# The last LayerNorm's weight and bias split by columns between VectorE and GpSimd

## What is computed

```python
def layer_norm(x, g, b):
    xf = x.astype(jnp.float32)
    mu = xf.mean(-1, keepdims=True)
    var = jnp.square(xf - mu).mean(-1, keepdims=True)
    return ((xf - mu) * lax.rsqrt(var + LN_EPS) * g.astype(jnp.float32) + b.astype(jnp.float32)).astype(x.dtype)
...
    x = layer_norm(ALPHA * x + moe(x, w_router, router_bias, w_exp_gu, w_exp_down, w_sh_gu, w_sh_down),
                   ln2_g, ln2_b)
```

## Time and profile before

| what | value |
|---|---|
| median of 3 runs | 2234.34 us (2234.02 to 2237.89) |
| the profiled execution | 2235.89 us |
| its span | 2234.1 us |
| busy in the span: TensorE, VectorE, ScalarE, GpSimd | 2070.3, 1078.4, 505.5, 550.4 us |
| last TensorE work ends, about | 2177.5 us into the span |
| the stage of the change | 2190.9 to 2230.0 us into the span |

### The profile page before, as it was taken

How to read it: one execution, slowest core, us unless ns; L and a number is a source line. 1 busy time by engine, 2 the same in 40 slices (tenths; PEclk the granted TensorE clock), 3 DMA queues, 4 the chain that set the end, 5 groups by cost and what they waited for, 6 DMA issues and landing times.

```text
span 2234.1 us, 24260 instructions
## 1 busy us (share of the span) xinstructions
PE 2070.3 (93%) x8178; PEld 1165.8 (52%) x8178; DVE 1078.4 (48%) x2232; ACT 505.5 (23%) x1011; POOL 550.4 (25%) x964
## 2 busy tenths in 40 slices
PE   8999698999998999998999898999999999999990
PEld 6755265655564656556555454444444444444440
DVE  5205599999998578963145553111111111111115
ACT  2314442000023652022022200111111111111122
POOL 0088860100031000100032243122222222222224
PEclk9999899999998999998999999999999999999995
DMA  4160004101010002104412141799999999999995
GB/s 129 46 68 3 1 4 151 38 19 47 1 31 18 1 1 57 43 15 151 137 55 68 38 160 52 277 367 370 371 366 368 366 364 367 367 368 368 371 337 176
DMA packets 126739, 365.20 MB, mean 163 GB/s; under 512 B 30849, under 2 KB 78722, under 8 KB 108866
## 3 DMA queue, kind: packets, MB, share of 16 engines
q1 hardware_dynamic: 106066, 290.21, 35.0%
q0 software_dynamic: 20016, 72.88, 12.9%
q10 hardware_dynamic: 576, 1.05, 0.1%
HBM read 310.82 MB, written 53.04 MB: 163 GB/s over the span
## 4 chain that ended last, share of the span: by engine, by line
PE 60%; DVE 23%; POOL 6%; issue 6%; ACT 2%; DMA 2%; SPq 0%; POOLq 0%; DVEq 0%; ACTq 0%
PE psum L817 21%; PE psum L831 10%; DVE arena L1672 9%; DVE best L1671 8%; PE psum L683 8%; PE psum L701 6%; PE psum L809 3%; PE psum L754 3%; ACT arena L1241 2%; PE psum L618 2%; PE psum L637 2%; POOL sct L1100 2%; PE psum L604 2%; PE psum L745 2%; POOL arena L1102 2%
## 5 line engine op out<-in xcount | busy, mean ns | idle before, releaser
L1241 ACT ACTIVATE arena<-psum 128x256 f32<-128x256 f32 (+8 forms) x714 | 334.4, 500 | 1517.8 <-PE psum L817 445.3
L817 PE MATMUL psum<-arena 128*128 128x512 f32 x1088 | 480.4, 594 | 1.1 <-DVE arena L1953 1.1
L817 PEld LDWEIGHTS psum<-arena 128*128 128x128 f32 x1088 | 202.7, 191 | 230.6 <-issue 229.4
L545 PE MATMUL psum<-arena 128*128 128x384 f32 (+1 forms) x768 | 238.9, 472 | 13.9 <-DVE arena L1697 8.4
L1671 DVE MAX8 best<-arena 128x8 f32<-128x384 f32 (+6 forms) x224 | 246.6, 1101 | 6.1
L1958 DVE TENSOR_TENSOR arena<-arena,psum 128x256 f32<-128x256 f32 x68 | 28.6, 421 | 454.6 <-ACT arena L1241 454.6
L831 PE MATMUL psum<-arena 128*128 128x512 f32 x544 | 244.8, 593 | 0.5 <-ACT arena L1241 0.5
L1672 DVE MATCH_REPLACE8 arena<-best,arena 128x384 f32<-128x384 f32 (+6 forms) x224 | 242.8, 1084 | 0.0
L545 PEld LDWEIGHTS psum<-arena 128*128 128x128 f32 x768 | 145.6, 191 | 106.8 <-DVE arena L1697 15.8
L1200 POOL TENSOR_TENSOR carry<-ones 1x1 f32<-1x1 f32 x135 | 52.1, 386 | 568.2 <-DVE arena L1967 521.1
L683 PE MATMUL psum<-arena 128*128 128x384 f32 (+1 forms) x576 | 179.1, 474 | 5.8 <-DMA arena<-in_w_attn_proj 5.8
(11 more groups left out here) (249 smaller groups left out, 2351.2 us busy)
## 6 DMA issues: line engine op xcount, KB each, us to landing
arena<-in_w_exp_gu SPq DMA_DIRECT2D x69, 2048.0 KB, 8.8
arena<-in_w_exp_down SPq DMA_DIRECT2D x68, 1024.0 KB, 7.4
arena<-in_w_in SPq DMA_DIRECT2D x24, 512.0 KB, 4.5
arena<-in_x_prompt SPq DMA_DIRECT2D x10, 512.0 KB, 4.1
arena<-in_w_glu SPq DMA_DIRECT2D x16, 256.0 KB, 5.0
arena<-in_w_attn_proj SPq DMA_DIRECT2D x16, 256.0 KB, 4.6
arena<-in_w_out SPq DMA_DIRECT2D x1, 4096.0 KB, 13.0
x_d<-arena SPq DMA_DIRECT2D x8, 512.0 KB, 2.9
```

Source lines behind the costliest of these rows:

```text
L545: last = mm(psum[:, b, 0:n], wgs[:, d % 2, w0 + k, :], src[:, k, t0:t0 + n], start=k == 0, stop=k == nk - 1)
L817: last = mm(psum[:, 2, :], xgT[u][:, k, :], ewg[u][:, k, :], start=k == 0, stop=k == DK - 1)
L1241: return act.activation(dst, src, fn, **kw)
```

## The change

The nine multiplies on VectorE and the nine adds on GpSimd, over all 1024 columns each, go. In their place VectorE does multiply and add on columns 0 to 383 of each tile (`weight_left`), and GpSimd does multiply and add on columns 384 to 1023. Both wait for `normed`, not for each other; each has a `step` between its two operations. SyncE waits for `out_left` and `out_right` before it stores a tile.

```diff
--- before.py
+++ after.py
@@ -78,6 +78,7 @@
 MASK_W = sum(keys(j)[1] for j in range(NT))
 TOK_CHUNKS = [(0, 384), (384, 384), (768, 320)]
 CHOOSING = list(range(2, NT))
+BY_VECTOR = 384
 
 
 class Banks:
@@ -1046,7 +1047,8 @@
                 ld(x1[0:rows(i), i, :], acc_d[tok(i), :], f"acc_loaded{i}")
 
             for i in range(NT):
-                sp.wait_ge(s("out_ready"), i + 1)
+                sp.wait_ge(s("out_left"), i + 1)
+                sp.wait_ge(s("out_right"), i + 1)
                 ld(out["y_p"][0, tok(i), :] if i < NT - 1 else out["y_s"][0], x1[0:rows(i), i, :], "out_stored")
             sp.wait_ge(s("out_stored"), 16 * NT)
             sp.wait_ge(s("v_stored"), 16 * NT)
@@ -1230,9 +1232,10 @@
 
             pool.wait_ge(s("ln2_loaded"), 32)
             for i in range(NT):
-                y = x1[0:rows(i), i, :]
-                pool.wait_ge(s("scaled"), i + 1)
-                tt(y, y, ln2[0:rows(i), 1, :], ALU.add).then_inc(s("out_ready"), 1)
+                r, y = rows(i), x1[0:rows(i), i, BY_VECTOR:]
+                pool.wait_ge(s("normed"), NT + i + 1)
+                step(tt(y, y, ln2[0:r, 0, BY_VECTOR:], ALU.mult))
+                tt(y, y, ln2[0:r, 1, BY_VECTOR:], ALU.add).then_inc(s("out_right"), 1)
 
 
         @block.scalar
@@ -1988,12 +1991,13 @@
                 dve.wait_ge(s(f"acc_loaded{i}"), 16)
                 variance(x, r, NT + i)
 
-            def scale_by_weight(i):
-                x = x1[0:rows(i), i, :]
+            def weight_left(i):
+                r, x = rows(i), x1[0:rows(i), i, 0:BY_VECTOR]
                 if i == 0:
                     dve.wait_ge(s("ln2_loaded"), 32)
                 dve.wait_ge(s("normed"), NT + i + 1)
-                tt(x, x, ln2[0:rows(i), 0, :], ALU.mult).then_inc(s("scaled"), 1)
+                step(tt(x, x, ln2[0:r, 0, 0:BY_VECTOR], ALU.mult))
+                tt(x, x, ln2[0:r, 1, 0:BY_VECTOR], ALU.add).then_inc(s("out_left"), 1)
 
             for i in range(NT + 2):
                 if i < NT:
@@ -2001,7 +2005,7 @@
                 if 0 <= i - 1 < NT:
                     scale_shift(rows(i - 1), NT + i - 1)
                 if 0 <= i - 2 < NT:
-                    scale_by_weight(i - 2)
+                    weight_left(i - 2)
 
 
 # ---- launch: one core; inputs and outputs as the reference has them ----
```

## The result

| | before | changed |
|---|---|---|
| median of 8 runs each, us | 2236.11 (2232.89 to 2241.6) | 2244.70 (2237.38 to 2248.83) |
| profiled execution, us | 2235.89 | 2245.38 |
| span, us | 2234.1 | 2243.5 |
| last stage, from tile 0's norm to the last operation, us | 35.45 | 40.30 |

The ratio is 1.0033, with a 95% interval of 1.0017 to 1.0048: slower by 7.4 us (3.8 to 10.7), where the forecast was 5.1 slower, a time of 2239.4 and a range up to 2242.4. The sign is right, the measured time lies 2.3 us above the range.

The account below looks back on a forecast made before the run. The prediction took GpSimd to set the last LayerNorm's pace by holding VectorE's one-column SCALAR_TENSOR_TENSOR. Steady tiles +6.62 and tail -1.53 gave +5.1 us, 2241.0 against the profiled execution, 2239.4 after its 1.55 us excess over the median; range 2235.8 to 2242.4.

Parts of the forecast that it names:

- The stage: Last LayerNorm, from tile 0's norm to the last VectorE or GpSimd operation: +6.62 - 1.53 = +5.1 us.
- The request of the small instruction: One-column SCALAR_TENSOR_TENSOR asks for the port 0.24 us after the gap between GpSimd's passes closes; held through the add.
- The period: Time per steady tile of the last LayerNorm: 4.50 us against 3.57, GpSimd waiting for ScalarE's norm.
- The VectorE pair: VectorE's multiply and add on the left 384 columns run beside ScalarE's norm, hidden with 0.30 us to spare.
- The steady tiles: Seven periods from tile 0's norm to tile 7's in the last LayerNorm: a loss of +6.62 us.
- The tail: From tile 7's norm to the last operation: 9.04 us against 10.57, VectorE and GpSimd in turn, gain -1.53 us.
- a rule for VectorE instructions with two inputs: A VectorE instruction with two SBUF inputs and a GpSimd one reading SBUF exclude each other for the whole instruction.
- How the numbers follow: Closing step giving chances for the whole time: slower by over 0.2% 0.60, within 0.2% 0.37, faster 0.03.
- something elsewhere in the program or the scatter of the runs: Case outside the last LayerNorm's terms, with runs of 2234.02 to 2237.89 us before: chance 0.03.
- The port is packed: Rival: the one-column SCALAR_TENSOR_TENSOR always finds the gap between GpSimd's passes; +1.8 us, 2236.1; packed or partly packed, chance 0.23.
- No exclusive hold: Rival: VectorE and GpSimd each run at their own pace, period 3.36 us; -4.3 us, 2230.0; chance 0.03.
- Worse than the sum: Rival: GpSimd's 640-column operation at 1.66 us, or VectorE losing every final turn; +6 to +8 us; chance 0.11.

Follow-up runs that it names:

- 640: The changed kernel with VectorE taking 640 columns and GpSimd 384, against the kernel before: ratio 0.9984 (0.9975 to 0.9993), stage 32.45 us.
- 512: The changed kernel with 512 columns each on VectorE and GpSimd, against the kernel before: ratio 1.0003 (0.9991 to 1.0014), stage 36.08 us.
- 640, one input: VectorE 640 columns, GpSimd 384, one-column SCALAR_TENSOR_TENSOR rewritten as TENSOR_SCALAR, against the kernel before: ratio 0.9986 (0.9974 to 0.9998), stage 32.32 us.
- 704: The changed kernel with VectorE taking 704 columns and GpSimd 320, against the kernel before: ratio 0.9970 (0.9955 to 0.9985), stage 32.68 us.
- the padded one: The kernel before plus nine tiny memsets ending each of VectorE's and GpSimd's streams and a second wait per store: ratio 1.0005 (0.9993 to 1.0017).

## Why the prediction was wrong, and where it was right

**The stage: right.** GpSimd's operation at 640 columns was put at 1.53 us and measured 1.53. The request of the small instruction was put 0.24 us behind the gap between GpSimd's passes; it came 0.23 behind the second pass's start. The period was put at 4.50 and measured 4.51. The VectorE pair hides, with 0.30 us to spare forecast and 0.29 measured. The steady tiles were put at +6.62: +6.79; 0.08 of the rest lie in the first period, 4.58, and 0.09 in the other six.

**The tail: right in kind, 0.4 us off, and the order was another.** It was put at -1.53 and is -1.94. The last small instruction is not held (0.15 us), as the text said. But VectorE's multiply of tile 7 got the port ahead of GpSimd (2232.09 against 2232.13), so the last operation is GpSimd's, not VectorE's. And I had charged four turns of 1.53 + 0.40. A full turn takes 1.80, as the ends at 2235.85, 2237.65 and 2239.45 show: VectorE 0.41, and GpSimd 1.39 from VectorE's end, so 0.14 of the 1.53 seem to pass inside the wait.

Sum of the stage: +4.85 for a forecast of +5.1. The two parts missed by 0.17 and 0.41 us in opposite directions, so the sum is a little closer than they are.

One reading goes further than its rows. The prediction says that the earlier trace rows agree with a rule for VectorE instructions with two inputs. The TENSOR_TENSOR there does; the CAST has one input and was held too, which the rule as the prediction words it doesn't give. For the forecast this changed nothing, since the stage has no CAST.

**The step that failed is the last one, "How the numbers follow".** It gave "something elsewhere in the program or the scatter of the runs" a chance of 0.03, and the time was tied to the median of three runs, 2234.34. Two things came of that. First, the base: eight runs of the kernel before have a median of 2236.11, 1.8 us higher; the three comparisons after that gave 2235.4, 2236.9 and 2237.7. Second, the scatter of the changed kernel's own runs. In the result its median stands 8.6 us over that of before, 3.7 more than the stage explains. That makes up the whole miss of 5.3 us (2244.70 against 2239.4): 1.8 from the base, 3.7 beyond the stage, less 0.2 in the stage. Single executions of either program spread over 7 to 14 us within a comparison. The attention stage's length, which goes with TensorE's granted clock around 950 to 1030 us, makes up to 6.5 of that. So a median of eight runs is itself unsure by 1 to 2 us. The text had the clue, 2234.02 to 2237.89 in three runs, and made a range out of the stage's terms alone. A range for the time has to carry the scatter of both sides; with 3 us more on each end it would have held.

**What stays open.** The three comparisons of the changed kernel give differences of the means of +7.0, +6.6 and +5.5 us, weighted +6.2 with a standard error of 0.9. The stage accounts for +4.85. What is left, 1.4 plus or minus 0.9, is no more than chance would give. The whole times of the other splits don't settle it: they have the same instructions in the same order (but for the rewritten small one), and go beyond their stages by -0.6 us (640), +0.1 (512), 0.0 (640, one input) and -3.9 (704), each with an interval of 2.0 to 3.4 us on either side.

The traces show one difference ahead of the stage, though. From the first transposes of L413 to the first of L618 (L414 and L619 with the split) the five kernels without the split took 617.2, 617.2, 617.5, 617.6 and 617.9 us, the last of them the padded one. All eight executions with it took longer, 618.2 to 618.9, on average 1.2 us more, some 1500 us ahead of the edited instructions. Both groups do the same work there. So about 1.2 us of the remainder look real, as far as one profiled execution of each kernel can tell, and no run here shows their cause.

**The rivals.** "The port is packed": no small instruction of a steady tile reached the gap. "No exclusive hold": the instructions of tiles 1 to 7 were all held until GpSimd's end. "Worse than the sum" gave a time near the measured one, for reasons that didn't occur: GpSimd was not dearer and VectorE did not lose its turns.

## What to carry to other kernels

Where VectorE's two-input instructions and GpSimd's passes share a stage, add their durations on one resource and look at which instruction stands first behind the hold: a one-column operation on the way to the next tile's norm put GpSimd's 3.1 us and ScalarE's norm of 1.24 one behind the other. Of work split between these two, GpSimd should get about as much as fits into the time in which VectorE runs instructions that were seen to pass beside it, here 2 x 0.99 us beside 1.8 us of statistics and reciprocal. One tensor input alone is no warrant of that: look at the instruction's duration beside GpSimd and without it, as the CAST of the earlier trace rows shows. And before a range is given for a change of a few us in a kernel of 2.2 ms, the scatter of the runs has to be in it.

## What the runs showed of the hardware

- The operand form matters for the hold: the same one-column product takes 1.32 us as SCALAR_TENSOR_TENSOR with two tensor inputs and 0.21 us as TENSOR_SCALAR with a per-partition scalar, both beside a GpSimd pass. That doesn't make one input safe: a CAST of 8 columns with one input waited 1.74 us for a GpSimd add.
- A waiting GpSimd operation of 640 columns ends 1.39 us after VectorE lets go, where one that starts freely takes 1.53. VectorE's of 384 takes 0.41 instead of 0.56.
- With both engines always ready (the changed kernel's tail), they took the port strictly in turn, also between the last GpSimd pass of one tile and the first of the next.
- With the small instruction no longer held, the changed kernel's loop did not settle at the free period of 3.4 us: it alternated between 3.4 and 5.3 us.
